# A fused hybrid decoder layer on one core: x and weight loads interleaved, memory transposes between slices, attention's last transposes ahead of its last slice, first gathers paced

## The reference, cut to what matters

```python
# x: (1, 256, 2048), mem: (1, 256, 2048)
mix = hybrid_mixer(x, ...)        # x @ w_in (2048 x 6144), 8 stick-breaking heads and 8 differential
                                  # heads of 128, RMS norm per head, @ w_o (2048 x 2048)
x = layer_norm(ALPHA * x + mix)
q = x @ w_mq ; kv = mem @ w_mkv   # (2048 x 2048) and (2048 x 4096), 4 heads of 512
x = layer_norm(ALPHA * x + softmax(q k^T) v @ w_mo)
q = x @ w_pq                      # PEER: scores against 2 x 128 keys, top 16 of 256 pairs per head
a = gate * gelu(expert_u[idx] . x)
x = layer_norm(ALPHA * x + sum(a * expert_v[idx]))   # 128*128 experts, 8 heads x 16 picks per token
```

## Time and profile before

| | |
|---|---|
| median of 3 runs | 2392.91 us (2392.11 to 2396.0) |
| the profiled execution | 2392.88 us, its span 2391.1 us |
| PE busy | 2310.8 us, 97% of the span |
| DVE, ACT, POOL busy | 1678.1 (70%), 1105.7 (46%), 635.8 us (27%) |
| mean granted clock of TensorE | 0.988 |

### The profile page before, as it was taken

How to read it: one execution, slowest core, us unless ns; L and a number is a source line. 1 busy time by engine, 2 the same in 40 slices (tenths; PEclk the granted TensorE clock), 3 DMA queues, 4 the chain that set the end, 5 groups by cost and what they waited for, 6 DMA issues and landing times.

```text
span 2391.1 us, 45242 instructions
## 1 busy us (share of the span) xinstructions
PE 2310.8 (97%) x14770; PEld 2094.6 (88%) x14770; DVE 1678.1 (70%) x2628; ACT 1105.7 (46%) x1716; POOL 635.8 (27%) x425
## 2 busy tenths in 40 slices
PE   7999999999899979999999999999899999999996
PEld 7988799878797879999999999999788888888885
DVE  4444556655643547699999999997677767777556
ACT  4444455543443334344555455554444444444442
POOL 0000000000201020687877778675000000000100
PEclk9999999999899989999999999999999999999998
DMA  8788644565353655688888888887888878888763
GB/s 321 251 277 270 195 140 143 161 224 194 131 184 113 194 141 133 149 196 194 196 197 196 193 197 194 200 196 204 288 288 288 288 245 285 286 285 275 240 220 123
DMA packets 333365, 507.60 MB, mean 212 GB/s; under 512 B 69072, under 2 KB 216784, under 8 KB 325744
## 3 DMA queue, kind: packets, MB, share of 16 engines
q1 hardware_dynamic: 285856, 443.79, 61.3%
q0 software_dynamic: 46736, 62.17, 11.1%
q10 hardware_dynamic: 704, 0.75, 0.1%
HBM read 485.33 MB, written 21.23 MB: 212 GB/s over the span
## 4 chain that ended last, share of the span: by engine, by line
PE 94%; DVE 2%; DMA 1%; ACT 1%; issue 1%; POOL 0%; SPq 0%; DVEq 0%; ACTq 0%; POOLq 0%
PE ps L707 28%; PE ps L670 27%; PE ps L460 18%; PE ps L466 15%; PE ps L660 2%; DMA temps<-gates_scratch 1%; PE ps L608 1%; PE ps L626 1%; DVE split_ring L1221 0%; DMA region<-in_x_dram 0%; PE ps L644 0%; DVE parts L1213 0%; ACT parts L775 0%; ACT split_ring L792 0%; PE ps L539 0%
## 5 line engine op out<-in xcount | busy, mean ns | idle before, releaser
L1221 DVE TENSOR_TENSOR split_ring<-weight_ring,split_ring 128x1024 fp32r<-128x1024 f32 x288 | 353.1, 1233 | 364.7 <-ACT split_ring L792 356.6
L707 PE MATMUL ps<-parts,temp_parts 128*128 128x512 f32 x2304 | 545.5, 390 | 6.3 <-DVE parts L1570 6.2
L1164 POOL DMA_INDIRECT gates_scratch<-sb_gains x256 | 506.6, 1979 | 158.3 <-issue 100.4
L707 PEld LDWEIGHTS ps<-parts,temp_parts 128*128 128x128 f32 x2304 | 433.2, 188 | 98.2 <-DVE parts L1570 8.1
L670 PE MATMUL ps<-parts,u_hi 128*128 128x240 f32 x3904 | 477.1, 275 | 0.0
L792 ACT ACTIVATE split_ring<-weight_ring 128x1024 fp32r<-128x1024 f32 x288 | 302.8, 1059 | 367.1 <-PE ps L460 226.1
L670 PEld LDWEIGHTS ps<-parts,u_hi 128*128 128x128 f32 x3904 | 456.0, 188 | 0.0
L460 PE MATMUL ps<-split_ring,parts 128*128 128x512 f32 x1920 | 439.8, 391 | 5.6 <-DVE parts L1337 3.9
L460 PEld LDWEIGHTS ps<-split_ring,parts 128*128 128x128 f32 x1920 | 360.7, 188 | 81.0 <-DVE split_ring L1221 4.1
L977 ACT ACTIVATE u_hi<-u_turned 128x1024 fp32r<-128x1024 f32 x244 | 259.0, 1062 | 316.8 <-DVE u_turned L1428 256.3
L466 PE MATMUL ps<-parts,split_ring 128*128 128x256 f32 x3072 | 379.5, 286 | 12.4 <-DVE split_ring L1221 7.1
(11 more groups left out here) (222 smaller groups left out, 1409.4 us busy)
## 6 DMA issues: line engine op xcount, KB each, us to landing
u_raw<-in_peer_u_dram SPq DMA_DIRECT2D x1024, 128.0 KB
region<-in_peer_v_dram SPq DMA_DIRECT2D x256, 512.0 KB, 4.7
weight_ring<-in_w_in_dram SPq DMA_DIRECT2D x96, 512.0 KB, 5.1
weight_ring<-in_w_mkv_dram SPq DMA_DIRECT2D x64, 512.0 KB, 4.1
gates_scratch<-temps POOLq DMA_DIRECT2D x16, 1024.0 KB, 7.2
weight_ring<-in_w_o_dram SPq DMA_DIRECT2D x32, 512.0 KB, 4.3
weight_ring<-in_w_mq_dram SPq DMA_DIRECT2D x32, 512.0 KB, 3.7
weight_ring<-in_w_mo_dram SPq DMA_DIRECT2D x32, 512.0 KB, 3.7
```

Of the source, the lines that this page charges most:

```text
L707: m = nc.tensor.matmul(ps[:, 4 * t + q, :], e[:, c], v, start=first and n == 0, stop=False, skip_group_check=True)
L1164: pool.indirect_dma_start(gates_by_one, bass.IndirectOffsetOnAxis(ap=idx_all[:, j:j + 1], axis=0), gate_all[:, j:j + 1], None, compute_op= ...
L1221: nc.vector.tensor_tensor(w_lo[j % SPLIT], raw[j % RAW], w_hi[j % SPLIT].bitcast(F32), ALU.subtract).then_inc(lo_ready, 1)
```

## The change

- SP loads x in four quarters with two weight slices between each (before: two quarters, two slices, two quarters, fourteen slices).
- PE transposes quarter 0 of x, then does slice 0, quarter 1, slices 1 and 2, quarter 2, slices 3 and 4, quarter 3, and the rest. ACT and DVE follow in the same order.
- Panel 0 of a pair now goes to banks 2 and 3 and panel 1 to banks 0 and 1 in the projections by `w_in`, `w_o` and `w_mo` (`flip=1`).
- Each group of mem's transposes stands behind a slice of the last panel of `w_in`; only groups 6 and 7 come after the last slice. Waits for `turned_taken` and for the last but one panel are put into the attention body instead, and POOL's staging waits for one pair less.
- In the attention body the transposes of the differential heads' output stand ahead of slice 15, and `@ w_o` no longer waits for the last panel before it.
- Gathers 0, 1 and 2 wait for 3, 5 and 7 finished blocks of the last stage; the lines' DVE work starts 4 blocks later (LINE_FROM 8, SUM_FROM 58).

The diff, cut to its core:

```diff
-        LINE_FROM, SUM_FROM = 4, 54
+        LINE_FROM, SUM_FROM = 8, 58
...
-                    if first and j == 1:
-                        load_x(range(2, NP))
-
-            load_x(range(2))
+                    if first and j in (1, 3, 5):
+                        load_x([(j + 1) // 2])
+
+            load_x([0])
...
-            def panel(kind, s, pair, acts):
-                slices(kind, range(s * NS, (s + 1) * NS), pair, acts, s, 1)
+            def panel(kind, s, pair, acts, flip=0):
+                slices(kind, range(s * NS, (s + 1) * NS), pair, acts, s ^ flip, 1)
...
-            for g in range(8):
-                if g % 2 == 0:
-                    pe.wait_ge(x_landed[g // 2], 16)
-                turn(x_in, g, g)
-                if g == 3:
-                    pe.wait_ge(turned_taken, 4)
-                    slices("cols", range(2), 0, xT, 0, 1)
-            slices("cols", range(2, 4), 0, xT, 0, 1)
-            pe.wait_ge(turned_taken, 8)
-            rest_of_pair(0, xT)
-            section("cols", 1, 1, xT)
-            section("rows", 2, 4, xT)
+            def turn_x(q):
+                pe.wait_ge(x_landed[q], 16)
+                for g in (2 * q, 2 * q + 1):
+                    turn(x_in, g, g)
+
+            turn_x(0)
+            for j in range(NS):
+                pe.wait_ge(turned_taken, j + 1)
+                slices("cols", [j], 0, xT, 1, 1)
+                if j in (0, 2, 4):
+                    turn_x(j // 2 + 1)
+            panel("cols", 1, 0, xT, flip=1)
+            section("cols", 1, 1, xT, flip=1)
+            section("rows", 2, IN_PAIRS - 3, xT, flip=1)
+            panel("rows", 0, IN_PAIRS - 1, xT, flip=1)
             pe.wait_ge(mem_landed, 16)
-            for g in range(8):
-                turn(mem_in, g, 8 + g)
-            pe.wait_ge(turned_taken, 16)
+            for j in range(NS):
+                slices("rows", [NS + j], IN_PAIRS - 1, xT, 0, 1)
+                if j > 0:
+                    turn(mem_in, j - 1, 8 + j - 1)
+            turn(mem_in, 7, 15)
...
                 pe.wait_ge(oT_copied, b * 2 - 1 + CREDIT)
+                pe.wait_ge(proj_taken, 2 * MKV0 - 1 + CREDIT)
...
+                pe.wait_ge(turned_taken, 14)
...
+                pe.wait_ge(turned_taken, 16)
                 slices(kind, range(0, 4), pair, memT, 0, 0)
...
-                slices(kind, range(12, 16), pair, memT, 0, 0)
+                slices(kind, range(12, 15), pair, memT, 0, 0)
                 pe.wait_ge(o_normed, b * 2 + 2 + CREDIT)
                 for c in range(4):
                     m = nc.tensor.transpose(ps[:, 7, c * P:(c + 1) * P], df_n[:, c, :], ident[:, :])
                 m.then_inc(oT_ready, 1)
+                slices(kind, range(15, 16), pair, memT, 0, 0)
...
-            pe.wait_ge(proj_taken, 2 * WO0 + CREDIT)
-            section("rows", WO0, NP // 2, mixedT)
+            section("rows", WO0, NP // 2, mixedT, flip=1)
...
+            for g in range(6):
+                copy_turned(p0, 8, [g])
+                if g < 5:
+                    split_hi(last, [14 + g])
+            copy_turned(p0, 8, [6])
+            take("rows", df_v, BANK, last, 1, 0)
+            copy_turned(p0, 8, [7])
+            split_hi(last, [19])
...
-            pool.wait_ge(proj_taken, 2 * MKV0 + CREDIT)
+            pool.wait_ge(proj_taken, 2 * MKV0 - 2 + CREDIT)
...
-                if c >= 3:
+                if c < 3:
+                    pool.wait_ge(v_used, 8 * c + 12)
+                else:
                     pool.wait_ge(line_used, c - 2 + int(c - 3 >= LINES // 2))
...
-            split_lo(IN_PAIRS - 1, range(8, 20))
-            turned_lo((p0, p4), 8, range(8))
+            split_lo(IN_PAIRS - 1, range(8, 14))
+            for g in range(8):
+                turned_lo((p0, p4), 8, [g])
+                if g < 5:
+                    split_lo(IN_PAIRS - 1, [14 + g])
+            split_lo(IN_PAIRS - 1, [19])
```

More of the change, by code:

```diff
@@ L629, in _ @@
             pe.wait_ge(co_copied, KB // 2)
-            section("rows", MO0, NP // 2, coT)
+            section("rows", MO0, NP // 2, coT, flip=1)
             pe.wait_ge(keys_landed, 16)
@@ L812, in section @@
                     split_pair(i + first_pair,
[L813 to L817, removed]
+                               lambda s: take(kind, dst, (i * 2 + s) * width, i + first_pair, s, 2 - 2 * s))
+            copy_turned(p0, 0, range(2))
+            split_hi(0, range(2), start=True)
+            copy_turned(p0, 0, range(2, 4))
+            split_hi(0, range(2, 4), start=True)
+            split_hi(0, [4])
+            copy_turned(p0, 0, range(4, 6))
+            split_hi(0, range(5, 7))
+            copy_turned(p0, 0, range(6, 8))
+            split_hi(0, [7])
             act.wait_ge(roped, 1)
             nc.scalar.activation(lam_e, lam_s, ACT.Exp).then_inc(roped, 1)
-            section("cols", r1, 0, 2, 2 * BANK)
+            for pair in range(2):
+                for s in range(2):
+                    split_hi(pair, range(4 + 8 * s if pair + s else 8, 11 + 8 * s))
+                    take("cols", r1, (2 * pair + s) * 2 * BANK, pair, s, 2 - 2 * s)
+                    split_hi(pair, [11 + 8 * s])
             section("rows", sb_v, 2, 1)
             section("rows", df_qk, 3, 2)
-            section("rows", df_v, 5, 1)
-            copy_turned(p0, 8, range(8))
+            last = IN_PAIRS - 1
+            split_hi(last, range(4, 11))
+            take("rows", df_v, 0, last, 0, 2)
+            split_hi(last, range(11, 14))
+            for g in range(6):
[6 more added lines that the diff above has]
+            split_hi(last, [19])
             def attention_body(b, kind):
@@ L880, in attention_body @@
                                      ACT.Copy).then_inc(oT_hi, 1)
+                take(kind, dst, i * 2 * width + width, pair, 1, 0)
+                split_hi(pair, [19])
             act.preload_act_table_set("natural_log_exp_and_others")
@@ L891, in _ @@
             copy_turned_whole(p1, 16, whole)
-            section("cols", r0, MQ0, NP // 2, 2 * BANK)
+            for i in range(NP // 2):
+                split_pair(i + MQ0, lambda s: take("cols", r0, (i * 2 + s) * 2 * BANK, i + MQ0, s, 2 * s))
             for h in range(MH):
@@ L1222, in split_lo @@
                                             ALU.subtract).then_inc(lo_ready, 1)
-            for n in range(2):
-                turned_lo((p0, p4), 0, range(4 * n, 4 * n + 4))
-                split_lo(0, range(2 * n, 2 * n + 2))
+            turned_lo((p0, p4), 0, range(2))
+            split_lo(0, range(2))
+            turned_lo((p0, p4), 0, range(2, 4))
+            split_lo(0, range(2, 5))
+            turned_lo((p0, p4), 0, range(4, 6))
+            split_lo(0, range(5, 7))
+            turned_lo((p0, p4), 0, range(6, 8))
+            split_lo(0, [7])
             dve.wait_ge(small_landed, 64)
@@ L1240, in _ @@
             steps.did(nc.vector.tensor_scalar(neg_lam, neg_lam, -LAMBDA_INIT, None, ALU.add))
-            with dve.Fori(0, IN_PAIRS - 1) as pair:
+            split_lo(0, range(8, 20))
+            with dve.Fori(1, IN_PAIRS - 1) as pair:
                 split_lo(pair, range(4, 20))
@@ L1330, in attention_body @@
                 mixed_rests(b, 0, 2)
-                split_lo(pair, range(16, 20))
+                split_lo(pair, range(16, 19))
                 mixed_rests(b, 1, 7)
+                split_lo(pair, [19])
             def mixed_rests(b, kind, src_bank):
```

8 lines of the change are left out of this document (3 added, 5 removed).

## The result

| | before | after |
|---|---|---|
| median of the runs on one chip | 2393.54 us (6 runs) | 2373.79 us (6 runs, 2371.18 to 2379.64) |
| profiled execution | 2392.88, span 2391.1 | 2375.05, span 2373.3 |
| mean granted clock | 0.988 | 0.989 |

The ratio of the times is 0.9917, with a 95% interval of 0.9903 to 0.9931: 19.7 us faster, where 21.4 were forecast.

A forecast was written before the change was run, and what follows sets the result against it. PE bounds the kernel, busy 2310.8 of 2391.1 us, so only its idle time or low clock can shrink. 4.3 + 4.6 + 5.4 + 7.1 = 21.4 us off 2392.9 gives 2371.5; 8-in-10 range 2367.5 to 2380.5.

The forecast's parts named there:

- start: Program start: first slice at 11.9 instead of 14.53 and no stall before slice 2; gain 4.3 us, bounds 1.8 to 5.5.
- w_in to attention: Step from w_in's last slices to attention's first: interleaved transposes of mem remove waiting; gain 4.6 us, bounds 4.0 to 4.9.
- attention to w_o: Step into w_o: PE's 3.86 us wait and the 1.6 us of low clock go; gain 5.4 us, low bound 3.9.
- gathers: First blocks of the last stage: pacing shrinks the first stall and removes the second; gain 7.1 us, bounds -1 to 8.5.
- The start does not move: Rival at the program start: the start gains 1.8 instead of 4.3 us, time 2374.0; chance 0.10.
- The memory step: From w_in to attention: gain 4.6 us, about 3.5 us from last slice to attention; its rival, not won, 2376.1, chance 0.06.
- a new wait stands where the transposes were put: Sign that the prediction is wrong: PE waits anew at the places the transposes were moved to; no size given.
- Attention waits in each body: Rival in attention: transposes ahead of slice 15 hold PE four times; 2393.1 or 2398, slower than before; chance 0.04.
- Two signs named in advance: Last stage: blocks 4 and 5 start 5.5 to 7 us after the one before, with no half clock there.
- the gates' landing at about 1678.8 instead of 1680.7, so 1.4 of the 3.2 stay: Last stage, first stall: with pacing the gates land sooner and 1.4 us of the 3.2 us stall remain.
- the rival on the narrow copies: Last stage: narrow copies alone hold the gates; first stall stays, half the second (2.6); gain 2.7 us, 2375.9; chance 0.20.

The follow-up runs named there:

- e9: The changed kernel with SP's order of loads alone put back as before, the engines' order kept new; 2375.89 us, ratio 0.9924.
- e7: The changed kernel with all of mem's transposes behind w_in's last slice again, new waits and banks kept; 2375.57 us, ratio 0.9921.
- e8: The changed kernel with attention's last transposes behind slice 15 again, the flips kept; 2376.73 us, ratio 0.9925.
- e4: The changed kernel with DVE's wait for the reload of x moved to its first use; 2371.79 us, ratio 0.9907.
- e1: The changed kernel with gathers 0 to 2 not paced and the lines' DVE work at its old blocks; 2377.61 us, ratio 0.9928.
- e2: As e1, but POOL fills the lines' x with zeros in place of the eight narrow copies; 2374.12 us, ratio 0.9911.
- e10: As e6, with the copies within DRAM issued earlier, in a quiet stretch; 2368.83 us, ratio 0.9896.
- e6: As e4, with the eight narrow copies replaced by copies within DRAM and one load of 128 partitions; 2372.25 us, ratio 0.9907.
- e11: As e10, with the pacing of the gathers taken back; 2374.03 us, ratio 0.9915.

## Why the prediction was right, and where it was not

| step | forecast | traces |
|---|---|---|
| start | 4.3 | 5.25 (113.68 to 108.43 at the end of the "cols" slices, from the chain) |
| w_in to attention | 4.6 | 4.5 (298.67 to 288.88, less the start's share) |
| attention to w_o | 5.4 | 3.7 (753.58 to 740.11 at w_mo: 13.5 in all) |
| gathers | 7.1 | 4.8 (19.40 to 14.61 us for blocks 4 and 5) |
| sum | 21.4 | 18.3, and 17.8 between the spans |

The small rest is some 0.3 us before the last stage and a late load of gates with 0.2 us of waiting behind it.

The measured 2373.79 lies 2.3 us above the forecast of 2371.5 and inside its range. The total came that near in part by luck. The start gave 1 us that was not foreseen, against 1.7 and 2.3 us that were missing in the last two steps, and the medians lie 1.9 us further apart than the traces that show the steps.

**The start** went as told, with one thing better. The prediction gave weight slice 0 the place and the time (9.44) of x's second quarter. It landed at 8.44, issued at 1.33 as x's second quarter was before, and of the same size. Why it came 1.0 us sooner is not known. The first slice started at 10.92 where 11.9 were told, and slice 7 ended at 39.3 (30.68 and three slices) where 40.0 were told. e9 shows that the order of the loads is 2.8 us of the gain. "The start does not move" is refuted.

**The memory step** has the forecast size (3.6 us from the last slice to attention, 3.5 were told). Its working made one sum of the interleaving and the moved waits. By e7 the interleaving is 2.1 us of it, and the moved waits, with what went along with them, 2.4.

**Attention to w_o.** Both parts that were priced came true: e8 brings back 3.86 us of idle time and the clock of 0.64 behind it. That is 3.8 us in the traces with the new stall of 1.5 us gone at the same time, so 5.3 where 5.4 were given. What failed is the question of what would be late next. DVE has a wait for the reload of x (`z_landed`) ahead of the residual loop, and behind it in its queue stand the remainders of all further weight slices. The load took 10.5 us in both kernels. DVE had stood for it in before too:

```profile
526.48 1.23 DVE L1221 TENSOR_TENSOR split_ring<-weight_ring,split_ring 128x1024 fp32r<-128x1024 f32 x1 [7.03 <-DMA region<-in_x_dram]
```

There it was issued at 515.79, PE began w_o at 519.79, and four slices in hand (4 x 2.73) lasted to 530.7: hidden, with 3 us to spare. After, it is issued at 506.57, PE has begun at 506.3, and the four slices end at 517.5, when the load has just landed and DVE's 1.24 us of work on the next slice is still to do. It was one of the signs named in advance ("a new wait stands where the transposes were put"), though it stands a few slices behind them. e4 shows it by removing it: 87.33 us instead of 88.8 for the section. "Attention waits in each body" did not happen: slices 12 to 14 take 8.64 us in the first two bodies and 8.22 in the others, which is three slices of 2.88 and 2.74 with no wait.

**The gathers.** The mechanism was right in both halves: e1 shows that the pacing removes the second stall, and e2 that the narrow copies make the first. Two signs named in advance failed, though: block 5 starts 9.16 us after block 4 and not 5.5 to 7, and there is a half clock there. The size of the rest was wrong: the step "the gates' landing at about 1678.8 instead of 1680.7, so 1.4 of the 3.2 stay". The gates came 3.36 us behind the start of block 4 in before (1680.76 less 1677.40) and come 2.29 behind it now (1666.52 less 1664.23), 1.1 us sooner where 1.9 were told. They were issued at 1656.92 and took 9.6 us. PE's wait fell from 2.90 to 1.83 us, but the 18 matmuls behind it now ran for the most part at the low clock (granted clock 0.50 in 1668.5 to 1670), 5.97 us where 4.24 is usual. The stall cost 3.7 us, more than before, and the working had no term for that. The first gather, at 1665.28, came too late to be the cause. The copies alone fill the queue, as this answer on the DMA traffic in 1656 to 1658 of after shows (queue, kind: packets, MB, share of 16 engines):

```profile
q0 software_dynamic: 71, 0.31, 93.6%
```

POOL's queue holds 93.6% of the engines for 0.31 MB. Over the whole transfer, the eight narrow copies in after (1653 to 1665) and the one wide load in e10 (1650 to 1661) compare like this:

```profile
q0 software_dynamic: 255, 1.05, 45.6%
```

```profile
q0 software_dynamic: 144, 1.05, 26.3%
```

For the same 1.05 MB the narrow copies took 5.5 us of all 16 engines (45.6% of 12), the wide load 2.9 (26.3% of 11). The reading behind the rival on the narrow copies is thus true for the first stall and false for the second, which its price of 2.6 us had kept. The Trainium skill, "SBUF — State Buffer", section "Door 1: The DMA port swizzle", ties a DMA's rate to the ports that its partitions reach. The runs agree as far as they go: copies to 16 partitions at a time stall the gates, and one load to 128 partitions of the same 1 MB (e6, e10) does not. They do not single out the ports, since that load is also one DMA where there were eight.

**What stays open.** The last stage of e4, e7, e8 and e9 is that of after, and its block 4 lost 2.1, 2.9, 1.6 and 2.0 us there, against 3.7 in after, by one profile each. Of the five, after's alone ran at the low clock behind the wait. So the term's 4.8 us holds for one execution, and by the others it would be 5.6 to 6.9, still under the 7.1 forecast: the rest of the first stall was put too low (1.4) in any case. Nor was it tried which part of the 2.4 us in e7 is the waits' and which POOL's staging, and the interleaving was not timed without them.

## What to carry to other kernels

When a stall in front of a stage goes, look for the next semaphore wait on each engine that feeds the stage, with the time of the DMA behind it: a wait placed ahead of a loop for convenience becomes a stall as soon as the engine gets there earlier. Here copies to 16 partitions at a time held the DMA engines nearly twice as long for the same bytes as one load to 128, and delayed a small, urgent load beside them; lay such data out in DRAM in a quiet stretch and bring it in with one load over all partitions. Pacing large transfers and widening narrow ones solve different stalls: with pacing alone (after) and with width alone (e11) one stall was left, and with both (e6, e10) none among the first blocks.

## What the runs showed of the hardware

TensorE's clock after a short wait did not follow the wait's length alone. 18 matmuls of 512 columns behind a wait took 4.37 to 4.42 us at the full clock (2.4 GHz) after 1.35 (e8), 1.67 (e9), 1.79 (e4), 2.54 (e7) and 3.17 us (e1) of idle time. They took 5.93 to 6.00 us, for the most part at the lower level (1.2 GHz), after 1.83 (after), 2.98 (e1) and 3.71 us (e11). The windows from 1664 to 1668 of e4 and from 1667.5 to 1671.5 of after:

```profile
1664.00:1668.00 4.00, 2.71 (x12) 2.26 (x13) 3.21 (x7) 2.60 (x5) 0.05 (x1) 1.00 1.06 413
```

```profile
1667.50:1671.50 4.00, 3.91 (x10) 3.10 (x11) 2.98 (x7) 2.23 (x5) 0.00 (x0) 0.57 0.97 350
```

So a stall has two prices, itself or itself and some 1.6 us more, and which of them it takes could not be told from these rows.
